# Attention block: square sums and key spreads in pairs on parts of the array, and a new order around the heads

## What is computed

```python
def _mla_mixer(h, cos, sin, w_in, q_a_norm, kv_a_norm, w_q_up, w_kv_up, q_norm, k_norm, w_out):
    p = h @ w_in
    c_q, c_kv, k_pe = jnp.split(p, (Q_RANK, Q_RANK + KV_RANK), axis=-1)      # 384, 256, 64
    q = (_rmsnorm(c_q, q_a_norm) @ w_q_up).reshape(B, T, 8, 192)
    kv = (_rmsnorm(c_kv, kv_a_norm) @ w_kv_up).reshape(B, T, 8, 256)
    k_nope, v = kv[..., :128], kv[..., 128:]
    k = jnp.concatenate([k_nope, broadcast(k_pe to 8 heads)], axis=-1)
    q, k = _rmsnorm(q, q_norm), _rmsnorm(k, k_norm)        # per head, over 192
    q, k = rope on the last 64 of each head
    o = causal softmax attention(q, k, v)
    return o.reshape(B, T, 1024) @ w_out
```

## Time and profile before

| | before |
|---|---|
| median of 3 runs | 2562.99 us (2561.6 to 2563.48) |
| profiled execution | 2565.41 us, span of its instructions 2563.6 us |
| TensorE busy | 2503.0 us, 98% |
| VectorE, POOL, ScalarE busy | 1254.9, 1183.2, 868.7 us |
| mean granted TensorE clock | 0.994 |
| chain that ended last | PE 86%, POOL 7%, DVE 3%, ACT 2%, issue 1% |

### The profile page before, as it was taken

How to read it: one execution, slowest core, us unless ns; L and a number is a source line. 1 busy time by engine, 2 the same in 40 slices (tenths; PEclk the granted TensorE clock), 3 DMA queues, 4 the chain that set the end, 5 groups by cost and what they waited for, 6 DMA issues and landing times.

```text
span 2563.6 us, 36473 instructions
## 1 busy us (share of the span) xinstructions
PE 2503.0 (98%) x14069; PEld 1930.7 (75%) x14069; DVE 1254.9 (49%) x1571; ACT 868.7 (34%) x1176; POOL 1183.2 (46%) x583
## 2 busy tenths in 40 slices
PE   8999999899999999889999999999999999999999
PEld 6676777688888777777888887888887446788887
DVE  7999974533322489655333223333225665433301
ACT  5533353422222345235322223323224243323221
POOL 3799834344444457223444444444443202444443
PEclk9999999899999999999999999999999999999999
DMA  5222223233333332003333333333333301333232
GB/s 151 72 77 75 74 83 98 66 94 94 91 91 95 103 90 68 6 5 101 97 91 94 88 98 92 95 91 97 91 90 82 77 19 50 91 92 96 88 97 78
DMA packets 418658, 213.29 MB, mean 83 GB/s; under 512 B 16805, under 2 KB 416987, under 8 KB 418555
## 3 DMA queue, kind: packets, MB, share of 16 engines
q1 hardware_dynamic: 414475, 209.05, 28.4%
q10 hardware_dynamic: 4080, 2.83, 0.5%
HBM read 209.22 MB, written 2.10 MB: 82 GB/s over the span
## 4 chain that ended last, share of the span: by engine, by line
PE 86%; POOL 7%; DVE 3%; ACT 2%; issue 1%; DMA 0%; ACTq 0%; POOLq 0%; DVEq 0%
PE bank L339 23%; PE bank L336 23%; PE bank L332 23%; PE bank L1334 2%; PE bank L1337 2%; PE bank L1330 2%; POOL w_lo L312 2%; PE bank L2842 1%; PE bank L2755 1%; PE bank L2195 1%; POOL tmp L789 1%; POOL tmp L794 1%; POOL tmp L792 1%; POOL tmp L785 1%; POOL tmp L783 1%
## 5 line engine op out<-in xcount | busy, mean ns | idle before, releaser
L312 POOL TENSOR_TENSOR w_lo<-w_raw,w_hi 128x1024 fp32r<-128x1024 f32 (+3 forms) x420 | 983.4, 2342 | 1276.4 <-ACT w_hi L303 1268.7
L303 ACT ACTIVATE w_hi<-w_raw 128x1024 fp32r<-128x1024 f32 (+3 forms) x420 | 425.1, 1012 | 1366.6 <-PE bank L339 1199.7
L332 PE MATMUL bank<-hH,w_hi 128*128 128x512 f32 x1712 | 442.9, 400 | 3.5 <-ACT w_hi L303 2.5
L336 PE MATMUL bank<-hL,w_hi 128*128 128x512 f32 x1712 | 436.6, 396 | 1.6 <-DVE hL L378 1.6
L339 PE MATMUL bank<-hH,w_lo 128*128 128x512 f32 x1712 | 434.0, 395 | 0.0
L332 PEld LDWEIGHTS bank<-hH,w_hi 128*128 128x128 f32 x1712 | 320.6, 188 | 90.9 <-issue 11.4
L336 PEld LDWEIGHTS bank<-hL,w_hi 128*128 128x128 f32 x1712 | 321.9, 188 | 82.3 <-DVE hL L378 3.8
L339 PEld LDWEIGHTS bank<-hH,w_lo 128*128 128x128 f32 x1712 | 320.9, 187 | 78.3
L527 DVE TENSOR_TENSOR tmp<-bank,R 128x512 f32<-128x512 f32 x88 | 60.9, 692 | 396.3 <-PE bank L339 396.2
L533 DVE TENSOR_TENSOR ffn_aL<-tmp,ffn_aH 128x512 f32 (+1 forms) x88 | 155.8, 1770 | 86.2 <-ACT ffn_aH L496 86.2
L332 PE MATMUL bank<-ffn_aH,w_hi 128*128 128x512 f32 x704 | 179.8, 395 | 0.0
(11 more groups left out here) (495 smaller groups left out, 2745.8 us busy)
## 6 DMA issues: line engine op xcount, KB each, us to landing
w_raw<-in_ffn_w_gate SPq DMA_DIRECT2D x88, 512.0 KB, 3.7
w_raw<-in_ffn_w_up SPq DMA_DIRECT2D x88, 512.0 KB, 3.7
w_raw<-in_ffn_w_down SPq DMA_DIRECT2D x64, 512.0 KB, 3.8
w_raw<-in_w_in SPq DMA_DIRECT2D x48, 512.0 KB, 3.8
w_raw<-in_even_w_in SPq DMA_DIRECT2D x26, 512.0 KB, 3.9
w_raw<-in_ffn_w_down SPq DMA_DIRECT2D x32, 384.0 KB, 3.4
w_raw<-in_w_conv_out SPq DMA_DIRECT2D x8, 512.0 KB, 3.9
w_raw<-in_w_out SPq DMA_DIRECT2D x8, 512.0 KB, 3.9
```

The source lines that it names most:

```text
L303: nc.scalar.activation(w_hi[u % 2][:, 0:K, :], w_raw[u % 4][:, 0:K, :], ACT.Identity).then_inc(w_hi_ready, 1)
L312: nc.gpsimd.tensor_tensor(w_lo[u % 2][:, 0:K, :], w_raw[u % 4][:, 0:K, :], w_hi[u % 2][:, 0:K, :].bitcast(F32), ALU.subtract).then_inc(w_l ...
L332: nc.tensor.matmul(out, H[:, k, :], sH[:, k0 + k, :], start=start and k == 0, stop=False)
L336: nc.tensor.matmul(out, H[:, k, :], sL[:, k0 + k, :], start=False, stop=False)
```

## The change

What is changed, in the order of the lists:

- `sel`, `selp` and the new `sel_pe` are 32 columns wide. The sum of head h goes to row h // 2 of partitions 0 to 31 (even h) or 32 to 63 (odd h), that is to column group h % 2 of the array. Two heads are summed together, at every second m (`head_sums`), except m = 8 to 11, where each sum now is two matmuls, one for each of the two heads in the tile. The squares get four buffers.
- The rope keys' sum is two matmuls, one for each half.
- The roots, their reciprocals, the copy and the transposes of the sums cover 64 partitions.
- The key spreads use 32 rows of `rk8`, 0 to 31 or 32 to 63, and run in pairs at m = 13, 15, 17 and 19; so do the `k_scale` pairs.
- ScalarE copies bank 4 before the next head's exponentials of tiles 3 and 2, and bank 6 after them. VectorE makes `o_lo` of h-1 behind the normalisation of h.
- The first output unit is taken apart: its high products with heads 0 to 5 run where TensorE has no scores left, ahead of head 7's transposes; the rest behind PV of head 7, with the products of head 7 last of each kind.

```diff
-        sel = a.put("sel", [P, 8, 8])
-        selp = a.put("selp", [P, 4, 8])
+        sel = a.put("sel", [P, 4, 32])
+        selp = a.put("selp", [P, 2, 4, 32])
+        sel_pe = a.put("sel_pe", [P, 32])
...
-                if m_ >= 3:
-                    act.wait_ge(mla["ss_mm"], sum_no(m_ - 3))
-                s.activation(tmp[m_ % 3][:, :], bank_of(u)[:, :], ACT.Square).then_inc(mla["sq"], 1)
+                if m_ >= 4:
+                    act.wait_ge(mla["ss_mm"], sum_no(m_ - 4))
+                s.activation(tmp[m_ % 4][:, :], bank_of(u)[:, :], ACT.Square).then_inc(mla["sq"], 1)
...
             for h in range(AH_):
-                if h + 1 < AH_:
-                    exps(h + 1, TILE_ORDER[:2])
                 for part, (b_, lo_, hi_) in enumerate(((4, PTO[0], PTO[1]), (6, PTO[2], TRI[TT]))):
+                    if part and h + 1 < AH_:
+                        exps(h + 1, TILE_ORDER[:2])
                     act.wait_ge(mla["t_ps"], 3 * h + (1, 3)[part])
...
-                if m_ >= 12:
+                if m_ >= 13 and m_ % 2:
+                    k_scale(m_ - 13)
                     k_scale(m_ - 12)
 
             v.wait_ge(mla["ss_mm"], 21)
-            V.tensor_copy(tmp[5][0:8, :], bank[4][0:8, :]).then_inc(mla["qs_rd"], 1)
+            V.tensor_copy(tmp[5][0:64, :], bank[4][0:64, :]).then_inc(mla["qs_rd"], 1)
...
+            def o_low(h):
+                v.wait_ge(mla["o_hi"], h + 1)
+                V.tensor_tensor(oL[:, h, :], bank[7][:, :], oH[:, h, :].bitcast(F32), S).then_inc(mla["o_lo"], 1)
...
                     V.tensor_scalar(p_, p_, rs[:, TT * h + i:TT * h + i + 1], None, M).then_inc(mla["pnorm"], 1)
+                if h:
+                    o_low(h - 1)
                 if h + 1 < AH_:
                     maxes(h + 1, TILE_ORDER[:2])
...
                     maxes(h + 1, TILE_ORDER[2:])
-                v.wait_ge(mla["o_hi"], h + 1)
-                V.tensor_tensor(oL[:, h, :], bank[7][:, :], oH[:, h, :].bitcast(F32), S).then_inc(mla["o_lo"], 1)
+            o_low(AH_ - 1)
...
-                    ins = mm(out, ident[0:8, i:i + 1].to_broadcast([8, P]), rk8[0:8, :], start=True, stop=True)
+                    r_ = slice(32 * (i % 2), 32 * (i % 2) + 32)
+                    col = 32 * (i % 2) + i // 2
+                    ins = mm(out, ident[r_, col:col + 1].to_broadcast([32, P]), rk8[r_, :], start=True, stop=True)
...
                 pe.wait_ge(mla["sq"], m_ + 1)
-                if m_ < 8:
-                    b_, lhs = bank[5], sel[:, m_, :]
-                elif m_ < 12:
-                    b_, lhs = bank[4], selp[:, m_ - 8, :]
+                s_ = tmp[m_ % 4][:, :]
+                if 8 <= m_ < 12:
+                    mm(bank[4][0:32, :], selp[:, 0, m_ - 8, :], s_, start=m_ == 8, stop=False)
+                    ins = mm(bank[4][32:64, :], selp[:, 1, m_ - 8, :], s_, start=m_ == 8, stop=False)
                 else:
-                    b_, lhs = bank[4], sel[:, m_ - 12, :]
-                mm(b_[0:8, :], lhs, tmp[m_ % 3][:, :], start=m_ in (0, 8), stop=m_ == 19).then_inc(mla["ss_mm"], 1)
+                    b_, h = (bank[5], m_) if m_ < 8 else (bank[4], m_ - 12)
+                    r_ = slice(32 * (h % 2), 32 * (h % 2) + 32)
+                    ins = mm(b_[r_, :], sel[:, h // 2, :], s_, start=m_ < 2, stop=m_ >= 18)
+                ins.then_inc(mla["ss_mm"], 1)
...
-                if m_ >= 1:
+                if 9 <= m_ < 13:
                     head_sum(m_ - 1)
+                elif m_ >= 2 and m_ % 2 == 0:
+                    head_sums(m_ - 2)
                 if m_ == 8:
-                    mm(bank[5][0:8, :], bones[:, 64:72], pe_sq[:, :], start=False, stop=True).then_inc(mla["ss_mm"], 1)
+                    mm(bank[5][0:32, :], sel_pe[:, :], pe_sq[:, :], start=False, stop=True)
+                    mm(bank[5][32:64, :], sel_pe[:, :], pe_sq[:, :], start=False, stop=True).then_inc(mla["ss_mm"], 1)
...
-                if m_ >= 12:
+                if m_ >= 13 and m_ % 2:
+                    side("key", m_ - 13)
                     side("key", m_ - 12)
-            head_sum(19)
+            head_sums(18)
...
+            out_ps_, out_hi, out_lo = bank_of(U_OO)[:, :], w_hi[U_OO % 2], w_lo[U_OO % 2]
+
+            def out_high(c0, c1, first=False):
+                if first:
+                    pe.wait_ge(w_hi_ready, U_OO + 1)
+                    pe.wait_ge(mla["exp"], turn_no(AH_ - 1, G_OF[U_OO] % 4))
+                for c in range(c0, c1):
+                    pe.wait_ge(mla["o_hi"], c + 1)
+                    nc.tensor.matmul(out_ps_, out_hi[:, c, :], oH[:, c, :], start=c == 0, stop=False)
+
+            def out_low(c0, c1):
+                for c in range(c0, c1):
+                    pe.wait_ge(mla["o_lo"], c + 1)
+                    nc.tensor.matmul(out_ps_, out_hi[:, c, :], oL[:, c, :], start=False, stop=False)
+                if c0 == 0:
+                    pe.wait_ge(w_lo_ready, U_OO + 1)
+                for c in range(c0, c1):
+                    ins = nc.tensor.matmul(out_ps_, out_lo[:, c, :], oH[:, c, :], start=False, stop=c == AH_ - 1)
+                if c1 == AH_:
+                    ins.then_inc(unit_done, 1)
+
             for h in range(AH_):
                 if h + 1 < AH_:
                     scores(h + 1, TILE_ORDER[:2])
+                else:
+                    out_high(0, AH_ - 2, True)
...
-            for j in range(8):
-                unit(pe, U_OO + j, 8, oH, oL, ready=(mla["o_lo"], 0) if j == 0 else None)
+            out_high(AH_ - 2, AH_ - 1)
+            out_low(0, AH_ - 1)
+            out_high(AH_ - 1, AH_)
+            out_low(AH_ - 1, AH_)
+            for j in range(1, 8):
+                unit(pe, U_OO + j, 8, oH, oL)
```

## The result

| | before | after |
|---|---|---|
| median | 2562.3 us (4 runs, 2560.39 to 2563.48) | 2540.16 us (4 runs, 2539.78 to 2540.6) |
| profiled execution | 2565.41 us, span 2563.6 us | 2539.78 us, span 2538.0 us |
| ratio | | 0.991, 95% interval 0.9897 to 0.9924 |

The kernel is 22.1 us faster. Two later sets of executions of the changed kernel (e4, e10) have medians of 2540.99 and 2541.95 us, both inside the range.

The account below looks back on a forecast made before the run. TensorE was taken to bound the unit loop and, apart from short waits, the head loop. Savings of 10.7 + 0.5 + 6.3 + 2.8 = 20.3 us off the median 2562.99 gave 2542.7 us, range 2540.5 to 2548.5.

Parts of the forecast that it names:

- sums and spreads in pairs: Unit loop: a pair of sums or key spreads costs what one does; 10.7 us saved, waits included.
- the wait before v(3): Unit loop: TensorE would reach v(3) before VectorE's copy of v(1) and wait about 1.0 us.
- first head: Head loop: the first head, which waited a shorter time (0.4 to 0.5), would save 0.5 us.
- six heads: Head loop: the new order brings a head from 8.70 to 7.65 us, saving 6.3 us over six.
- last head and first output tile: End of head loop: six high products fill the wait ahead of head 7's transposes; 2.8 us saved, bounds 1.4 and 3.0.
- The visit's price: Unit loop: one visit to the narrow 128x8 shape costs 1.14 us, 0.86 streaming and 0.28 going in and out.
- the ring: Head loop: the chain over ScalarE and VectorE from transposes to transposes, forecast at 6.5 us, under TensorE's 7.6.
- A: Rival, sums: column pairs run in turn, costing 12.4 us more than forecast, 2555.1 us; chance 4%.
- B: Rival, head loop: stays bound over ScalarE and VectorE, the copy blocking ScalarE's queue; 3.2 us lost, 2545.9 us; chance 14%.
- C: Rival, unit loop: VectorE becomes the bound there; 3 us lost, 2545.7 us; chance 12%.
- D: Rival, head loop: ScalarE's copy blocks so long that the kernel gets slower, 2566 us at 11.5 us a head; chance 2%.
- E: Rival, whole kernel: pairs and waits cancel, time within 5 us of before; chance 2%.

Follow-up runs that it names:

- e4: The whole change once more, on the same chip as its three parts, against the kernel before: median 2540.99 us against 2563.50.
- e10: The whole change again, on another chip, against the kernel before: median 2541.95 us against 2563.96, ratio 0.9914.
- e1: Kernel before with only the paired sums and spreads, head loop and output units unchanged: median 2552.79 us, against 2563.50 for the kernel before.
- e8: Changed kernel with VectorE's copy of v(1) ahead of the query latent's reciprocal and scalings: one execution, 2538.96 us.
- e5: Kernel before with only ScalarE's copy of bank 4 put ahead of the next head's exponentials: one execution, 2553.80 us.
- e6: Kernel before with only VectorE's o_lo of h-1 put behind the normalisation of h: one execution, 2556.73 us.
- e9: Kernel before with ten needless matmuls in the idle gap ahead of head 7's transposes: median 2562.90 us, ratio 0.9997.
- e7: Changed kernel with the four rope sums made in two visits instead of four, same matmuls: one execution, 2540.61 us.

## Why the prediction was wrong by a little

| term | forecast | by the traces |
|---|---|---|
| sums and spreads in pairs, with the wait before v(3) | 10.7 | 11.0 (e1 11.01) |
| first head | 0.5 | 0.64 |
| six heads | 6.3 | 7.2 |
| last head and first output tile | 2.8 | 2.85 |
| sum | 20.3 | 21.7 |

**The pairs.** Right. Column pairs overlap, as the earlier trace rows had it, and the strict reading of the Trainium skill ("TensorE: Matmul & The Clock Gate", Part 3, where weight loads overlap running matmuls only across row groups) does not hold for two column groups here: the halves of a rope sum start 0.01 us apart, and the weight loads for their second records stand at 2003.84 and 2003.85, while the first records run until 2004.27. The visit's price held in the sum of the loop, with 6.64 us for the forecast 6.59; the wait before v(3) was there, 0.66 (e8) for the forecast 1.0, which is the term's error: VectorE's copy of v(1) came 1.4 us sooner than before and not 1.1, since the three scalings ahead of it took 2.08 us where they had taken 2.38. At the end of the loop the copy of the sums and TensorE's scores are ready within 0.1 us of each other, as forecast.

**The head loop.** The mechanism was right: both edits cut the ring, and TensorE binds behind them. The normalisation is done at 2064.47, 1.15 us before the transposes start. The step that failed is the size: "TensorE binds, at 7.60 to 7.94; I take 7.65". It came out at 7.48, below the lower of two ends that were meant to enclose it. The 7.60 was pieced together from a head that waited twice, 1.24 us for transposes and 2.32 for PV; e5 and e6 show each of these 0.06 to 0.07 us longer behind a wait. 0.12 us of the 0.17 a head is that, and the rest is the 0.05 that I put on top. The earlier trace rows held the waits, and the first head of the kernel before, whose transposes didn't wait, had 1.19 us for them: it was there to be read. The 7.94 counted the modelled ends of matmuls as work.

**The last head.** Right: the transposes start 1.57 us behind the end of PV(6) (1.5 forecast), and 2.85 us go.

**The rest.** 21.7 against 20.3 explains 1.4 of the 2.5 us. The other 1.1 us are not in the trace of the attention. 0.7 us of them belong to the kernel before: the forecast was taken off its median of three executions, 2562.99 us, and with a fourth the median is 2562.3. The last 0.4 is the saving of 22.1 by the medians against 21.7 by the traces. Three times the changed kernel was measured, with medians of 2540.16, 2540.99 and 2541.95 us, and before had 2562.3, 2563.5 and 2563.96, so the saving is 22.1, 22.5 and 22.0, some 0.3 to 0.8 us beyond the traces. The slow clock behind the idle time of before (e1, e5) would do that and has the right size, and e9 fits it without proving it; chance would do it too, since medians of few runs move by about a microsecond, for which the range had nothing at its lower end. With the terms as measured the forecast would have been 2541.3 us, inside the range, so that the time fell outside it is partly chance. The lower end should have been a wait-free head, and that scatter below it.

**The rivals.** A is refuted by the trace (pairs within 0.01 us). B by the 7.48 us of a head and by e5: the copy, put first, blocks nothing. C is true in its places and small in its sum: 0.66 us at v(3), and 1.08 us before v(6), only 0.35 more than the 0.73 of before. D and E did not come near.

## What to carry to other kernels

Price TensorE's pieces from a place where nothing waits. A group behind a wait carries more than the wait that the profile names, so pieces from a waiting loop bound the wait-free loop from above, not from both sides. When two edits cut the same ring, measure each: one alone brought 0.95 and the other 0.52 of the 1.22 us, and neither alone reached TensorE's own time. And reshaping small sums into pairs pays for the streaming saved and for every change of shape that goes with it.

## What was not expected of the hardware

- A float32 sum into 8 or 32 columns between units costs 0.86 us of streaming and about 0.28 us of changing shape, and two sums in one visit pay the latter once (1.84 us against 2 x 0.98, e7, and the next product without its own 0.1).
- An idle time of 2.81 us behind a loop with shorter ones was followed in two of three profiles by a lower granted clock (0.67 over 2121 to 2126 us in e5, 0.78 and 0.79 in the two windows from 2118 to 2126 in e1), which made transposes and PV 1.3 us slower. In none of the ten profiles with at most 1.5 us of idle time there did it happen, and the changed kernel has no such gap.
- Two float32 matmuls of a column pair, each of two records, interleave: the first records of both start within 0.01 us, and so do the second records, 0.43 to 0.46 us later, though the program has the two matmuls one behind the other. On two row groups it is the same with 0.53 us.
